# A hybrid MLA and gated-linear-attention step on one core: norm sums, latent scaling, key rope and first splits issued in earlier stages

## What is computed

```python
cq, ckv, kr, gq, gk, gv, gr, gg = jnp.split(x @ w_in, idx, axis=-1)
q = (rms_norm(cq, q_norm) @ w_uq).reshape(B, T, MLA_HEADS, MLA_NOPE + MLA_ROPE)
q_nope, q_rope = q[..., :MLA_NOPE], q[..., MLA_NOPE:]
q_rope = apply_rope(q_rope, cos[:, None, :], sin[:, None, :])
k_rope = apply_rope(kr, cos, sin)          # one key for all four heads
ckv = rms_norm(ckv, kv_norm)
...
s = (einsum('bqhr,bkr->bhqk', q_lat, ckv) + einsum('bqhe,bke->bhqk', q_rope, krope)) * MLA_SCALE
...                                        # causal softmax; GLA: chunked recurrence of q, k, v, decay
gla = rms_norm(gla_o, gla_norm) * silu(gg)
y = post_block(x, concat([mla, gla]) @ w_out, ...)   # layer norms, squared-ReLU MLP
```

## Time and profile before

| | us |
|---|---|
| timed executions, median of 3 | 1293.06 |
| lowest and highest | 1288.5, 1295.41 |
| the profiled execution, own time | 1285.75 |
| its span, first to last instruction | 1283.7 |
| TensorE busy in it | 1228.5 |
| VectorE busy | 821.1 |
| ScalarE busy | 561.4 |
| GpSimd busy | 171.1 |

### The profile page before, as it was taken

One profiled execution on the slowest core, in us unless ns is written; L12 is line 12 of the kernel. 1 busy time (PEld: TensorE's weight loads), 2 busy tenths in 40 slices (PEclk: granted clock), 3 DMA queues, 4 the chain that ended last, 5 costly groups with the idle time before them and its releaser, 6 DMA issues. The chain is left out here.

```text
span 1283.7 us, 24507 instructions
## 1 busy us (share of the span) xinstructions
PE 1228.5 (96%) x9666; PEld 1167.3 (91%) x9666; DVE 821.1 (64%) x1292; ACT 561.4 (44%) x927; POOL 171.1 (13%) x217
## 2 busy tenths in 40 slices
PE   6999998999899999999999999999999999999996
PEld 6988777999768888999999999999999999999995
DVE  4122222344797777675987787777658566668977
ACT  4312323233655547454654444444474223332435
POOL 3614443110000000132000000000000000000652
PEclk9999999999899999999999999999999999999998
DMA  8759888533311012522146877867597654554103
GB/s 291 226 160 295 272 282 282 183 100 99 110 58 48 1 50 72 188 72 81 61 170 242 304 264 250 307 248 281 202 324 273 212 175 166 192 198 152 46 26 108
DMA packets 116536, 226.92 MB, mean 177 GB/s; under 512 B 13203, under 2 KB 60581, under 8 KB 114118
## 3 DMA queue, kind: packets, MB, share of 16 engines
q1 hardware_dynamic: 110278, 208.57, 47.9%
q0 software_dynamic: 6144, 16.79, 4.2%
HBM read 165.54 MB, written 58.73 MB: 175 GB/s over the span
## 5 line engine op out<-in xcount | busy, mean ns | idle before, releaser
L2848 PE MATMUL psum<-step_hid_hi,step_w_hi 128*128 128x258 f32 x784 | 158.3, 283 | 1.4 <-DVE y_sums L2887 1.4
L2848 PE MATMUL psum<-step_hid_hi,step_w_lo 128*128 128x258 f32 x784 | 157.8, 283 | 0.0
L2848 PE MATMUL psum<-step_hid_lo,step_w_hi 128*128 128x258 f32 x784 | 157.3, 282 | 0.0
L355 PE MATMUL psum<-xTh,win_hi 128*128 128x344 f32 (+1 forms) x432 | 146.7, 340 | 9.7 <-DVE xTl L408 9.7
L355 PE MATMUL psum<-xTh,win_lo 128*128 128x344 f32 (+1 forms) x432 | 138.7, 321 | 0.0
L355 PE MATMUL psum<-xTl,win_hi 128*128 128x344 f32 (+1 forms) x432 | 138.6, 321 | 0.0
L2848 PEld LDWEIGHTS psum<-step_hid_hi,step_w_hi 128*128 128x128 f32 x784 | 122.1, 190 | 1.6 <-DVE step_w_lo L2823 1.6
L2848 PEld LDWEIGHTS psum<-step_hid_hi,step_w_lo 128*128 128x128 f32 x784 | 121.4, 190 | 0.0
L2848 PEld LDWEIGHTS psum<-step_hid_lo,step_w_hi 128*128 128x128 f32 x784 | 120.9, 189 | 0.0
L2465 PE MATMUL psum<-x_t_hi,w_variant_hi 128*128 128x258 f32 x512 | 103.8, 284 | 5.2 <-DVE hid_variants L2582 2.9
L2810 ACT ACTIVATE step_hid_hi<-step_hid_raw 128x2064 fp32r<-128x2064 f32 x21 | 40.6, 1934 | 149.6 <-PE psum L2848 132.5
(11 more groups left out here) (424 smaller groups left out, 2988.5 us busy)
## 6 DMA issues: line engine op xcount, KB each, us to landing
step_hid_raw<-hid_rows SPq DMA_DIRECT2D x21, 1032.0 KB, 7.5
k_pages<-in_pages SPq DMA_DIRECT2D x128, 160.0 KB, 3.1
v_pages<-in_pages POOLq DMA_DIRECT2D x128, 128.0 KB, 4.7
w_raw<-in_w SPq DMA_DIRECT2D x16, 1024.0 KB, 5.0
hid_rows<-hid_variants SPq DMA_DIRECT2D x28, 516.0 KB, 3.0
step_w_raw<-w_sums SPq DMA_DIRECT2D x12, 1024.0 KB, 5.2
hid_rows<-hid_variants SPq DMA_DIRECT2D x14, 774.0 KB, 5.1
step_w_raw<-in_w SPq DMA_DIRECT2D x9, 1024.0 KB, 5.2
```

Source lines behind the costliest of these rows:

```text
L355: mm = pe.matmul(psum[0:M, 3 * (m % 2) + b, 0:BLK], w[:, m % 2, k, 0:M], x[:, k, b * BLK:(b + 1) * BLK], start=(k == 0 and i == 0), stop=( ...
L2848: mm = pe.matmul(slot(d)[:, s, :], wt[r][:, w], ht[r][:, TH * f + s * BW:TH * f + (s + 1) * BW], start=(f == 0 and i == 0), stop=(f == G - ...
```

## The change

What it does, part by part:

- **Norm sums in the projection.** After each of the tiles 0 to 4 ScalarE squares it from `proj_stage` (`act_norm_squares`). VectorE adds at p = 7, 10 and 17 (`dve_norm_sum`). TensorE makes the column sums at p = 13 (`nq`) and 18 (`nk`), in the decode bank, ahead of the scores of that p. Both roots are made together at p = 34, with Ln and Exp and two Newton steps on VectorE. The scales of q are made there too. The memset of `grT` moves from the start to p = 18, because the squares use its place.
- **Latent scaling in GLA slots.** `bc` 0 and 1 are issued in slots 33 and 39, in the GLA banks, and VectorE scales ckv there.
- **Key rope in GLA slots.** The two products are in slot 41, the sum in slot 45. For this SP issues the swapped key behind cq and the rope tables when `so` 3 (slot 38) is done, both ahead of the head's weights.
- **First splits.** The first head's weights (high in slot 45, low in 47) and cq's first third (slot 48) are split earlier; ckv's halves follow cq's.
- **Order and banks of the set-up.** Transposes 3 to 7 are spread between other groups, the first rope passes are issued by thirds of cq, the first head's q and k move from banks 6 and 7 to the set-up's six banks, which start with bank 4, and q comes before the second swap.

Three places in the order of the instructions.

The core of the diff:

```diff
+        NQ_AT, NK_AT = 13, 18
+                if m < ROW_KR:
+                    act_norm_squares(act, m)
...
+        def act_norm_squares(act, m):
+            act.wait_ge(proj_out, m + 1)
+            if m in (2, 3):
+                act.wait_ge(nsum_done, m - 1)
+            if m == 4:
+                dq.wait(act, ("nq",))
+            act.activation(nsq[(0, 1, 1, 1, 0)[m]][:], pstage[:, m % 2, 0:TP], ACT.Square).then_inc(nsq_done, 1)
+
+        def dve_norm_sum(dve, i):
+            dve.wait_ge(nsq_done, (2, 3, 5)[i])
+            to, other = ((0, 1), (0, 1), (1, 0))[i]
+            if i == 1:
+                dve.wait_ge(nsum_done, 1)
+            dve.tensor_tensor(nsq[to][:], nsq[to][:], nsq[other][:], ALU.add).then_inc(nsum_done, 1)
...
             if p == GATE_LN_AT:
                 act_gate_ln(act)
+                act.wait_ge(rv_done, 2)
+                alink(act, act.activation(rstdc[:], rvar[:], ACT.Ln))
+                act.activation(rstdc[:], rstdc[:], ACT.Exp, scale=-0.5).then_inc(rr_done, 1)
...
-                   44: [("sO",)], 47: [("nk",)], 50: [("gT", 0), ("gT", 1)], 53: [("gT", t) for t in range(2, 5)]}
+                   33: [("bc", 0)], 39: [("bc", 1)], 44: [("sO",)], 50: [("gT", 0), ("gT", 1)], 53: [("gT", 2)]}
...
+            if s in (41, 45):
+                dve_krope(dve, s == 45)
+            if s == 47:
+                head_lo(dve, 0)
+            if s == SLOTS:
+                lo_of(dve, "cq0")
...
         def dve_gla(dve):
             for s in range(SLOTS, SLOTS + 3):
                 dve_slot(dve, s)
-            dve_rstd_rms(dve, 0)
-            dve.sem_inc(rk_done, 1)
-            lo_of(dve, "wr"), lo_of(dve, "cq0")
+            lo_of(dve, "wr"), lo_of(dve, "cq1")
...
-        mb = Banks("mla_setup_bank", [5, 0, 1, 2, 3, 4], M_TASKS)
+        mb = Banks("mla_setup_bank", [4, 5, 0, 1, 2, 3], M_TASKS)
...
         def pe_mla_in(pe):
             pe.wait_ge(proj_out, NT)
+            split(pe, "wr")
+            pe_rope_in(pe, 0, 0, (0,)), pe_rope_in(pe, 0, 1, (0,))
+            pe_gla_task(pe, ("gT", 3))
+            split(pe, "cq1")
+            pe_rope_in(pe, 0, 0, (1,)), pe_rope_in(pe, 0, 1, (1,))
             split(pe, "cq2")
+            pe_rope_in(pe, 0, 0, (2,)), pe_rope_in(pe, 0, 1, (2,))
+            pe_gla_task(pe, ("gT", 4))
+            pe_rope_in(pe, 1, 0)
             pe_rope_swap(pe, 0)
+            pe_rope_in(pe, 1, 1)
+            pe_gla_task(pe, ("gT", 5)), pe_gla_task(pe, ("gT", 6))
+            pe_first_head(pe, "q", 0), pe_first_head(pe, "q", 1)
+            pe_gla_task(pe, ("gT", 7)), pe_gla_task(pe, ("gTs",))
+            pe_rope_swap(pe, 1)
             split(pe, "ck1")
+            pe_first_head(pe, "k", 0), pe_first_head(pe, "k", 1)
             split(pe, "uv")
...
         def dve_mla_in(dve):
+            lo_of(dve, "ck1")
             dve_rope(dve, 0)
+            gated(dve, 5), gated(dve, 6)
             dve.wait_ge(gst_stored, 80)
             dve_head_part(dve, ("q", 0, 0))
+            lo_of(dve, "q0")
             dve_head_part(dve, ("q", 0, 1))
+            gated(dve, 7)
+            gated_sample(dve)
+            lo_of(dve, "uv")
             dve_rope(dve, 1)
+            lo_of(dve, "kr")
             dve_head_part(dve, ("k", 0, 0))
             dve_head_part(dve, ("k", 0, 1))
```

More of the change, by code:

```diff
@@ L606, in dve_decode @@
         def dve_decode(dve, p):
+            if p == 7:
+                dve_norm_sum(dve, 0)
+            if p == 10:
+                dve_norm_sum(dve, 1)
+            if p == 17:
+                dve_norm_sum(dve, 2)
+            if p in (NQ_AT, NK_AT):
+                key, i, n = (("nq",), 1, 3 * P) if p == NQ_AT else (("nk",), 0, 2 * P)
+                dq.wait(dve, key)
+                dq.free(dve.tensor_scalar(rvar[:, i, :], dq.of(key)[:, 0:8], 1.0 / n, EPS, ALU.mult, ALU.add), key)
+                dq.read(dve, key)
+                dve.sem_inc(rv_done, 1)
+                if p == NK_AT:
+                    dve.memset(grT[:], 1.0).then_inc(gr_ones, 1)
             if p == 8:
@@ L1611, in hymba_step, with head_bank @@
             "scores_full", "softmax_bias", "softmax_exp", "p_normed", "head_hi_part", "pT_hi_part"))
-        HI = [k for k in W_TASKS if k[0] != "pv"]
+        HI = [(kind, 0, b) for kind in "qk" for b in range(2)] + [k for k in W_TASKS if k[0] != "pv"]
+        def head_bank(h):
+            return wk if h else mb
         def sc_view(u):
```

277 lines of the change are left out of this document (120 added, 157 removed).

## The result

| | before | changed |
|---|---|---|
| timed executions beside each other, median, us | 1293.06 | 1279.16 |
| ratio of the two, 95% interval | | 0.9901 (0.9883 to 0.9918) |
| the profiled execution, own time | 1285.75 | 1279.16 |
| its span | 1283.7 | 1277.4 |
| all executions of the study with their clock: how many | 87 | 10 |

Faster, by 12.2 us on the means (13.9 between the two medians at the top), where 8.7 had been forecast. One of the five executions behind the median of 1279.16 us took 1496.77 us at a clock of 0.749; it is in no mean and in no ratio here.

The account below looks back on a forecast made before the run. TensorE, busy 96% of the span, bounds the kernel, so only its waits and slow clock count: -7.7 - 2.4 - 3.5 + 2.2 + 2.2 + 0.5 = -8.7 us, from 1293.06 to 1284.4, range 1278.5 to 1290.5.

Parts of the forecast that it names:

- Step 1: MLA set-up: the new order removes all of TensorE's waits for VectorE, 7.7 us off.
- Step 2: MLA set-up: TensorE's clock no longer falls to its lower level, 2.4 us off.
- The first rival: Set-up: the clock still falls, two new bank waits following one another; gain 6.3 us, time 1286.8, chance 0.12.
- Step 3: Set-up: norm sums leave, 3.5 us off; broadcasts leave and come back in GLA slots with 1.9 us, nothing gained.
- Step 4: Projection: added norm sums cost 1.8 us for q and 0.4 for k, 2.2 together, bounds 0 and 3.5.
- The sign named for this step: Projection's last score matmuls: moving by 0 or by 3.5 us instead of 2.2 would show the norm-sum price wrong.
- Step 5: End of GLA slots: two low halves ahead of VectorE's last mask make TensorE wait 1.7 and 0.5 us, 2.2 added.
- Step 6: GLA slot 41: krope products ahead of the Newton step add 0.5 us, bounds 0 and 3.
- the third rival: Slot 41: rope tables land late and hold VectorE; 8.8 us net loss, time 1301.9, chance 0.05.
- The second rival: Set-up: half of the 7.7 us of waits returns elsewhere, VectorE 91% busy; gain 4.8 us, time 1288.2, chance 0.20.

Follow-up runs that it names:

- a_again: The changed kernel once more, no edit; median 1280.16 us, ratio 0.9895 to the kernel before.
- a_nosums: The changed kernel without squares, sums and norm-sum matmuls in the projection, variances set to 1; median 1281.04 us, ratio 0.9930 to the kernel before.
- a_hid: The changed kernel with both sets of norm sums moved ahead of the ninth score; median 1282.36 us, ratio 0.9910 to the kernel before.
- a_load: The changed kernel with VectorE's old load put back as nine unused additions (9 us); median 1285.65 us, ratio 0.9953 to the kernel before.
- b_sums: The kernel before plus squares, sums and both sets of norm-sum matmuls in the projection, results unused; median 1294.76 us, ratio 1.0026.
- b_again: The kernel before once more, no edit; median 1291.05 us, ratio 0.9997.
- b_less: The kernel before in its old set-up order, with the work the change takes out of there left out altogether; median 1285.40 us, ratio 0.9951.
- b_fill: The kernel before plus twelve unused matmuls ahead of each of two waiting set-up transposes; median 1292.01 us, ratio 1.0003.

## Why the prediction was right, and where it was not

The mechanism is the one forecast: TensorE's waits for VectorE in the set-up go, the clock there stays up, and the added sums and the late mask take part of it back. The size was less well met. The gain of 13.9 us between the medians is beyond the 11.9 that the prediction gave as the upper end; the time lies inside the range only by the microseconds added for scatter. The bounds do not add up either: those of steps 4 to 6, taken together, allow a gain of 2.3 to 13.6 us, not 6.5 to 11.9. The first attention scores come 7.7 us earlier (380.5 against 388.2), where 9 was forecast.

**Step 1, waits of the set-up: right.** All 7.7 us are gone. The reason given, that it is what the queue does last and not how much, is half of it: load alone and order alone are worth 1 to 2 us each, both 6.6 to 7.3.

**Step 2, the slow clock: right in kind, too small.** No row of the set-up is below 1.00. The step priced the rows that it saw slowed, 2.4 us; the stretches give two falls of 1.7, 3.4, of which 0.6 lay in the second wait, so 2.8 us. More than that, the forecast counted falls in one execution. The timed executions of before lose 13.8 us to the clock on average (1289.4 x 0.0107) and those of the changed kernel 9.1; the profiled one of before lost 6.4. Each of these holds some 4 us behind the last matmul. The mean difference of 4.7, less the 2.4 forecast, is the largest part of what the forecast missed. 3.4 of it are the set-up's if every execution of before has its two falls there, as both profiles have; the rest I can't place.

**The first rival, clock still falls: wrong as a rule, true now and then.** The two new waits of 1.57 and 0.41 us stand where it put them, and the clock is 1.00 in the changed kernel, in `a_again` and in `a_nosums`. In `a_hid`, with the same two waits, one fall of 1.7 us followed them, and with a further wait of 3.3 us in `a_load` one came as well. By the rule of the Trainium skill cited in step 2 ("TensorE: Matmul & The Clock Gate", section "A second HAM failure mode: psum-queue depth-cycling"), such waits throw the clock back; these traces agree once in four.

**Step 3, norm sums and broadcasts out of the set-up: right.** `bc` comes back with 1.06 us a time in the slots, and the stretch of the slots grows by 1.8.

**Step 4, norm sums in the projection: the term that was sized too small.** "1.8 us paid" for q is right. "I take 0.4" for the k sums failed: later waits for pages did not give the rest back. 2.2 was forecast; 3.7 to 4.0 were measured over the profiles and 4.2 on the executions of `b_sums`, above the step's upper bound of 3.5. The sign named for this step would have missed it: the last scores come 5.5 us later, and without the two falls ahead of them 2.1. The waits for key pages scatter from 4.7 to 8.7 us between the profiles whose sums are not hidden behind them, so the earlier trace rows were one draw.

**Step 5, the low halves ahead of the mask: right rows, wrong price.** Waits of 1.57 and 0.41 us where 1.7 and 0.5 were forecast. But a wait is not a cost: with the halves moved, 0.5 us comes back. The step looked for who waits and did not ask what else VectorE would then do late.

**Step 6, krope in slot 41: right.** The wait for the state is 0.5 instead of 0.3 us. The tables came in time, so the third rival did not come about.

**The second rival, waits come back elsewhere: wrong.** Its mechanism, VectorE at 91%, is the state the kernel is in, and `a_load` shows that it was close.

**The sum.** Without the clock the forecast was 6.3 us, and 7.3 were measured (1275.6 to 1268.3): the set-up gave 10.3 (135.4 to 125.1 us less lost time, where -7.7, -3.5, 2.2 and 0.5 make 8.5), the projection took 3.7 instead of 2.2. Three terms were off by 1 to 2 us each and cancelled in part. The base moved it further: the median of three that the forecast started from is 1.7 us above the mean of 87.

## What to carry to other kernels

Read the granted clock of the timed executions before comparing a profile with them, and multiply it with the span: here up to 4.7 of the 12.0 us gained were clock. Before counting a wait as a cost, see whether its releaser has idle time on the same stretch; if it has none, moving the work only moves the wait, and what helps is less of it or doing it in an earlier stage where that engine idles. In this kernel the waits for pages, which scatter between executions, hid part of the sums that were put right ahead of them and next to nothing of those put several scores upstream.

## What was not expected of the hardware

- Up to TensorE's last matmul, the time lost to its clock comes in steps of 1.7 us, a spell of 3.4 us or a multiple of it at the lower of the two levels: 1.7, 3.4, 5.1, 6.8 and 10.2 us in the stretches of fourteen profiles.
- Many spells follow a wait of TensorE. Nine waits between its first and last matmul are 2.7 us or longer; in eight of the nine a spell begins in the wait or within 1 us behind it, also where it was a wait for key pages with no transposes near. The ninth, 3.3 us at 203 us in the profile of before, has none. Most of the waits of 1.5 to 2.2 us have none either. How long those waits are differs from execution to execution, and so does the number of spells.
- Other spells come without a wait. All but two of the fourteen profiles have one between 60 and 70 us, in or right behind a run of 72 rows of matmuls of 8 columns (4.3 us) during which TensorE is never idle; the two that have none are those of before and `b_again`, and `b_less` and `b_fill` have the same instructions up to there. The Trainium skill, "TensorE: Matmul & The Clock Gate", section "What's actually happening", says of a kernel's start that the same kernel makes more or fewer of its first matmuls at the lower clock from run to run; these profiles show such a difference in the middle of a kernel.
- Sixteen matmuls of one output column in a row had 3 and 2 falls in them or right behind them, with TensorE busy all the time; eight and eight, 13 us apart, had none in two profiles. That is four profiles, and shown no further.
- At the start of the attention, behind waits of 1.1 and 0.7 us that all kernels have, a fall came in four of the nine profiles with the new set-up and in one of the five with the old.
